# Three of a two-layer decoder kernel's buffers serve as extra slots for the last layer's expert weights, where one did before

## What is computed

```python
def memory_cross_attention(h, mem_n, wq, wkv, wo):
    ...
    s = jnp.einsum('bshd,bmhd->bhsm', q, k).astype(F32) * (X_DH ** -0.5)
    p = jax.nn.softmax(s, axis=-1)
    o = jnp.einsum('bhsm,bmhd->bshd', p, v.astype(F32)).reshape(B, S, D)
    return o.astype(h.dtype) @ wo

def hierarchical_moe(h, w_rg, w_re, w_gate, w_up, w_down):
    ...
    hg = jnp.einsum('nd,edf->nef', t, w_gate)
    hu = jnp.einsum('nd,edf->nef', t, w_up)
    act = (jax.nn.silu(hg.astype(F32)) * hu.astype(F32) * gates[..., None]).astype(t.dtype)
    y = jnp.einsum('nef,efd->nd', act, w_down)
```

## Time and profile before

| | us |
|---|---|
| median of 3 runs | 1109.47 |
| lowest and highest | 1107.93, 1112.87 |
| profiled execution, device time | 1111.42 |
| profiled execution, its span | 1109.5 |
| PE, DVE and ACT busy in the span | 1029.5, 397.4, 136.9 |

### The profile page before, as it was taken

The page is one execution under the profiler, slowest core; times in us unless marked ns, Lnnn a source line. Parts: engine busy times, 40 slices in busy tenths (PEclk is TensorE's granted clock), DMA queues, the critical chain, the costliest instruction groups (busy, mean ns, idle before and its releaser), DMA issues.

```text
span 1109.5 us, 10478 instructions
## 1 busy us (share of the span) xinstructions
PE 1029.5 (93%) x4366; PEld 559.1 (50%) x4366; DVE 397.4 (36%) x722; ACT 136.9 (12%) x303; POOL 58.0 (5%) x105
## 2 busy tenths in 40 slices
PE   6999999999978999999997999999996899988995
PEld 5666556577564443333333855566853433333332
DVE  5203455413133223333243324562124333333332
ACT  4010002302010001100111000041111000100001
POOL 3001111000010000000000101100000100000000
PEclk9999999999998999999998999999999899999998
DMA  8954423252156999999899344226403699999993
GB/s 344 429 223 152 152 84 147 76 195 109 34 215 228 380 429 426 411 428 410 366 425 427 131 152 152 76 79 227 151 2 152 246 431 426 426 426 429 426 426 133
DMA packets 25239, 293.54 MB, mean 265 GB/s; under 512 B 3296, under 2 KB 3552, under 8 KB 8544
## 3 DMA queue, kind: packets, MB, share of 16 engines
q1 hardware_dynamic: 19392, 266.40, 59.0%
q10 hardware_dynamic: 4640, 22.19, 5.2%
q0 software_dynamic: 1152, 4.19, 1.0%
HBM read 283.33 MB, written 9.44 MB: 264 GB/s over the span
## 4 chain that ended last, share of the span: by engine, by line
PE 81%; DMA 11%; DVE 4%; issue 2%; ACT 1%; DVEq 0%; POOL 0%; SPq 0%; ACTq 0%
PE bank L806 14%; PE bank L477 12%; PE bank L830 10%; PE bank L625 10%; PE bank L485 9%; DMA ring<-in_w_experts 8%; PE bank L496 5%; PE bank L498 5%; PE bank L836 4%; PE bank L554 3%; DMA late<-in_w_experts 2%; PE bank L467 2%; PE bank L677 1%; PE bank L690 1%; PE bank L706 1%
## 5 line engine op out<-in xcount | busy, mean ns | idle before, releaser
L806 PE MATMUL bank<-ring,hT 128*64 128x512 f32 x944 | 224.3, 594 | 11.7 <-DMA ring<-in_w_experts 9.8
L806 PEld LDWEIGHTS bank<-ring,hT 128*64 128x64 f32 x944 | 73.8, 137 | 144.1 <-issue 143.0
L477 PE MATMUL bank<-ring,hT 128*128 128x512 f32 x320 | 140.3, 592 | 0.0
L830 PE MATMUL bank<-ring,work 128*64 128x512 f32 x480 | 113.4, 595 | 6.5 <-ACT work L1039 3.2
L625 PE MATMUL bank<-ring,hT 128*128 128x512 f32 x256 | 112.1, 594 | 0.0
L485 PE MATMUL bank<-hT,ring 128*128 128x256 f32 x448 | 99.8, 385 | 2.1 <-DVE hT L1281 2.1
L477 PEld LDWEIGHTS bank<-ring,hT 128*128 128x128 f32 x320 | 59.6, 190 | 68.0 <-issue 67.9
L485 PEld LDWEIGHTS bank<-hT,ring 128*128 128x128 f32 x448 | 86.4, 194 | 14.7 <-DVE hT L1281 2.7
L1562 DVE TENSOR_TENSOR x<-bank,x 128x512 f32<-128x512 f32 x64 | 44.3, 692 | 137.3 <-PE bank L836 137.3
L625 PEld LDWEIGHTS bank<-ring,hT 128*128 128x128 f32 x256 | 48.0, 190 | 57.7 <-issue 56.8
L830 PEld LDWEIGHTS bank<-ring,work 128*64 128x64 f32 x480 | 36.4, 137 | 68.3 <-issue 58.4
(11 more groups left out here) (235 smaller groups left out, 977.9 us busy)
## 6 DMA issues: line engine op xcount, KB each, us to landing
ring<-in_w_experts SPq DMA_DIRECT2D x89, 2048.0 KB, 15.7
ring<-in_w_mix SPq DMA_DIRECT2D x30, 2048.0 KB, 9.2
late<-in_w_experts SPq DMA_DIRECT2D x7, 2048.0 KB, 20.8
late<-in_w_mix ACTq DMA_DIRECT2D x4, 2048.0 KB, 12.5
rot<-by_slot ACTq DMA_DIRECT2D x14, 512.0 KB, 10.5
by_slot<-late ACTq DMA_DIRECT2D x1, 4096.0 KB, 50.3
work<-in_mem SPq DMA_DIRECT2D x2, 512.0 KB, 4.4
x<-in_x SPq DMA_DIRECT2D x1, 1024.0 KB, 13.4
```

The lines of the kernel that those rows point to most:

```text
L477: last = nc.tensor.matmul(b[:, :], lhs[:, c, m * P:(m + 1) * P], w[:, c, :], start=(c == 0), stop=(c == C - 1))
L806: last = nc.tensor.matmul(banks[2 + g][b2 * CAP:(b2 + 1) * CAP, :], rowsT[p % 2][:, c, b2 * CAP:(b2 + 1) * CAP], w, start=(c == 0), stop=( ...
L830: last = nc.tensor.matmul(banks[5 + n][b2 * CAP:(b2 + 1) * CAP, :], ractT[:, c, b2 * CAP:(b2 + 1) * CAP], w, start=(c == 0), stop=(c == 3))
```

## The change

The diff makes `KT` and `memT` one buffer, `keys`, of exactly one slot's size, and lets the last layer's expert units use it as slot `KEYS`, and `work` as slot `WORK`. There are nine slots for these 48 units instead of seven: of each nine units the first goes to `late`, the sixth to `keys`, the seventh to `work`, the others round the ring. The first load into `keys` waits for the job `sx11`, the first into `work` for `pt11`. As `work` is no longer free in the last layer's experts, their temporaries lie in `Vx` there (and one of the dense branch in `rot`). In the first layer all stays where it was. The lines that do the same for the dense branch are left out.

```diff
@@ -35,7 +35,8 @@
 
 
 SLOTS = 6
-LATE = SLOTS
+LATE, KEYS, WORK = SLOTS, SLOTS + 1, SLOTS + 2
+LAST_SLOTS = {0: LATE, 5: KEYS, 6: WORK}
 UNITS = ["k0", "k1", "v0", "v1", "hf", "hq", "hi", "aq", "ak", "hg", "av", "o0", "o1", "q0", "q1", "p0", "p1"]
 KV_UNITS = 4
 PAIRS = N_EXPERTS // 2
@@ -109,11 +110,13 @@
 def unit_places():
 
 
+
     order = []
     for layer in range(DEPTH):
         order += [(layer, name, None) for name in UNITS[KV_UNITS if layer else 0:]]
-        n = SLOTS + (layer == DEPTH - 1)
-        order += [(layer, (j // 6, j % 6), LATE if n > SLOTS and j % n == 0 else None) for j in range(6 * PAIRS)]
+        more = LAST_SLOTS if layer == DEPTH - 1 else {}
+        n = SLOTS + len(more)
+        order += [(layer, (j // 6, j % 6), more.get(j % n)) for j in range(6 * PAIRS)]
     places, at, tenants = {}, 0, {}
     for layer, key, slot in order:
         if slot is None:
@@ -177,7 +180,8 @@
         x = sb("x", [P, M, D])
         xs = sb("xs", [P, M, D])
         hT = sb("hT", [P, C, T])
-        memT = sb("memT", [P, C, T])
+        keys = sb("keys", [P, 2, C, T])
+        memT, KT = keys[:, 0, :, :], keys[:, 1, :, :]
         late = sb("late", [P, 4 * M * W])
         hi = late[:, 0:M * W].rearrange("p (m n) -> p m n", m=M)
         gg = late[:, M * W:2 * M * W].rearrange("p (m n) -> p m n", m=M)
@@ -189,7 +193,6 @@
         S01 = PT[:, 2, 0:HG_HEADS, :]
         PT0 = PT[:, 0:2, :, :].rearrange("p a (h m) t -> p (a h) m t", m=M)
         PT1 = PT[:, 2, :, :]
-        KT = sb("KT", [P, 8, T])
         Vx = sb("Vx", [P, M, D])
         lev = sb("lev", [P, 8, P])
         bias0 = sb("bias0", [P, P])
@@ -236,7 +239,7 @@
         banks = [ctx.enter_context(nc.psum_tensor(f"bank{i}", [P, W], F32)) for i in range(8)]
 
 
-        loaded = [sem(f"loaded{s}") for s in range(SLOTS + 1)]
+        loaded = [sem(f"loaded{s}") for s in range(SLOTS + len(LAST_SLOTS))]
         kv_loaded, kv_done, kv_emptied = sem("kv_loaded"), sem("kv_done"), sem("kv_emptied")
         router_loaded = sem("router_loaded")
         late_reset = sem("late_reset")
@@ -318,7 +321,9 @@
             eng.wait_ge(empt[who], L * EMPTIED[who] + NTH[name])
 
         def slot_view(slot):
-            return ring[:, slot, :] if slot < SLOTS else late[:, 0:C * W]
+            if slot < SLOTS:
+                return ring[:, slot, :]
+            return {LATE: late[:, :], KEYS: keys[:, :, :, :].rearrange("p a c t -> p (a c t)"), WORK: E}[slot]
 
         def unit(name, L=0):
             return slot_view(PLACES[L, name][0]).rearrange("p (c n) -> p c n", c=C)
@@ -341,9 +346,12 @@
             tots.append(TOT[:, :, off:off + (T >> j)])
             off += T >> j
 
-        actb = work[:, 0, :].rearrange("p (m n) -> p m n", m=M)
-        actT = work[:, 1, 0:W].rearrange("p (c t) -> p c t", c=4)
-        gexp = work[:, 2, :].rearrange("p (m n) -> p m n", m=M)
+        def last(L):
+            return L == DEPTH - 1
+
+        actb_of = [(Vx[:, 0, :] if last(L) else work[:, 0, :]).rearrange("p (m n) -> p m n", m=M) for L in range(DEPTH)]
+        gexp_of = [(Vx[:, 1, :] if last(L) else work[:, 2, :]).rearrange("p (m n) -> p m n", m=M) for L in range(DEPTH)]
+        actT_of = [(rot[:, 0:W] if last(L) else work[:, 1, 0:W]).rearrange("p (c t) -> p c t", c=4) for L in range(DEPTH)]
         HALF_PI = float(np.pi / 2)
 
         logits = wsm[:, 0:40].rearrange("p (m n) -> p m n", m=M)
@@ -371,7 +379,9 @@
         by_slot = nc.dram_tensor("by_slot", (N_EXPERTS * CAP, D), F32, kind="Internal").ap()
         rowsT = [hT[:, :, 0:P], hT[:, :, P:T]]
         rows = [rot[:, 0:D], rot[:, D:2 * D]]
-        ract, ractT, rexp = work[:, 0, 0:W], work[:, 1, 0:W].rearrange("p (c t) -> p c t", c=4), work[:, 2, 0:W]
+        ract_of = [Vx[:, 0, 0:W] if last(L) else work[:, 0, 0:W] for L in range(DEPTH)]
+        rexp_of = [Vx[:, 1, 0:W] if last(L) else work[:, 2, 0:W] for L in range(DEPTH)]
+        ractT_of = [(Vx[:, 0, W:D] if last(L) else work[:, 1, 0:W]).rearrange("p (c t) -> p c t", c=4) for L in range(DEPTH)]
         yrows = PT[:, 2, :, :].rearrange("p h t -> p (h t)")
         hot = PT[:, 0, 0:2, :]
         gated = PT[:, 0, 2:4, :]
@@ -414,8 +424,8 @@
 
                 slot, _, had = PLACES[L, key]
                 if had is None:
-                    if slot == LATE:
-                        wait_job(sp, L, "ap1")
+                    if slot >= SLOTS:
+                        wait_job(sp, L, {LATE: "ap1", KEYS: "sx11", WORK: "pt11"}[slot])
                     return
                 l, old = had
                 if isinstance(old, tuple):
@@ -816,7 +826,7 @@
                         rows_transposes(p + 1, 0)
                     pe.wait_ge(r_act[L], p + 1)
                     for k in range(4):
-                        last = nc.tensor.transpose(banks[4][:, k * P:(k + 1) * P], ract[:, k * P:(k + 1) * P], ident[:, :])
+                        last = nc.tensor.transpose(banks[4][:, k * P:(k + 1) * P], ract_of[L][:, k * P:(k + 1) * P], ident[:, :])
                     routed_job(last)
                     if p + 1 < PAIRS:
                         rows_transposes(p + 1, 1)
@@ -827,7 +837,7 @@
                         for c in range(4):
                             for b2 in range(2):
                                 w = expert_unit(p, 4 + b2)[:, c * D + n * W:c * D + (n + 1) * W]
-                                last = nc.tensor.matmul(banks[5 + n][b2 * CAP:(b2 + 1) * CAP, :], ractT[:, c, b2 * CAP:(b2 + 1) * CAP],
+                                last = nc.tensor.matmul(banks[5 + n][b2 * CAP:(b2 + 1) * CAP, :], ractT_of[L][:, c, b2 * CAP:(b2 + 1) * CAP],
                                                         w, start=(c == 0), stop=(c == 3))
                         routed_job(last)
                     for n in range(2):
...
@@ -1032,11 +1042,11 @@
 
                 def routed(p):
                     act.wait_ge(r_jobs[L], ROUTED[p, "gate"])
-                    nc.scalar.activation(rexp, banks[2][:, :], ACT.Exp, scale=-1.0).then_inc(r_gexp[L], 1)
+                    nc.scalar.activation(rexp_of[L], banks[2][:, :], ACT.Exp, scale=-1.0).then_inc(r_gexp[L], 1)
                     act.wait_ge(r_jobs[L], ROUTED[p, "weights"])
                     nc.scalar.activation(gatedT, banks[7][:, 0:M * P].rearrange("p (m t) -> p m t", m=M), ACT.Copy).then_inc(r_evac[L], 1)
                     act.wait_ge(r_jobs[L], ROUTED[p, "act"])
-                    nc.scalar.activation(ractT, banks[4][:, :].rearrange("p (c t) -> p c t", c=4), ACT.Copy).then_inc(r_evac[L], 1)
+                    nc.scalar.activation(ractT_of[L], banks[4][:, :].rearrange("p (c t) -> p c t", c=4), ACT.Copy).then_inc(r_evac[L], 1)
                     if p + 3 < PAIRS:
                         act.wait_ge(r_jobs[L], ROUTED[p, "rows1"])
                         load_rows(p + 3)
...
@@ -1546,11 +1556,11 @@
 
                     taken(r_jobs[L], ROUTED[p, "gate"])
                     dve.wait_ge(r_gexp[L], p + 1)
-                    inner.link(V.tensor_scalar(rexp, rexp, 1.0, None, ALU.add))
-                    inner.link(V.reciprocal(rexp, rexp))
-                    inner.link(V.tensor_tensor(rexp, banks[2][:, :], rexp, ALU.mult))
+                    inner.link(V.tensor_scalar(rexp_of[L], rexp_of[L], 1.0, None, ALU.add))
+                    inner.link(V.reciprocal(rexp_of[L], rexp_of[L]))
+                    inner.link(V.tensor_tensor(rexp_of[L], banks[2][:, :], rexp_of[L], ALU.mult))
                     taken(r_jobs[L], ROUTED[p, "up"])
-                    V.tensor_tensor(ract, banks[3][:, :], rexp, ALU.mult).then_inc(r_act[L], 1)
+                    V.tensor_tensor(ract_of[L], banks[3][:, :], rexp_of[L], ALU.mult).then_inc(r_act[L], 1)
                     if p + 1 < PAIRS:
                         for c2 in range(2):
                             rows_transposed(p + 1, c2, ROUTED[p, f"rows{c2}"])
...
```

More of the change, by code:

```diff
@@ L859, in dense @@
                             for k in range(4):
-                                last = nc.tensor.transpose(banks[4][:, k * P:(k + 1) * P], actb[:, m, k * P:(k + 1) * P], ident[:, :])
+                                last = nc.tensor.transpose(banks[4][:, k * P:(k + 1) * P], actb_of[L][:, m, k * P:(k + 1) * P], ident[:, :])
                             last.then_inc(d_jobs[L], 1)
@@ L868, in dense @@
                                 for c in range(4):
-                                    last = nc.tensor.matmul(banks[5 + n][:, :], actT[:, c, :], w[:, c, n * W:(n + 1) * W],
+                                    last = nc.tensor.matmul(banks[5 + n][:, :], actT_of[L][:, c, :], w[:, c, n * W:(n + 1) * W],
                                                             start=(c == 0), stop=(c == 3))
@@ L1054, in dense @@
                             act.wait_ge(d_act[L], n4 + 2 * b2)
-                            nc.scalar.activation(gexp[:, m, :], banks[m][:, :], ACT.Exp, scale=-1.0).then_inc(d_gexp[L], 1)
```

(7 more changed lines are left out.)

## The result

| | before | changed |
|---|---|---|
| first measurement, median of 4 runs, us | 1110.65 (1107.93 to 1112.87) | 1100.89 (1099.52 to 1101.56) |
| ratio of the changed kernel to the one before | | 0.9909, 95% interval 0.9887 to 0.9931 |
| second measurement, median of 11 and of 6 runs, us | 1111.15 | 1102.24 (1099.26 to 1105.85) |
| its ratio | | 0.9922, interval 0.9898 to 0.9946 |
| profiled execution, device time and span, us | 1111.42, 1109.5 | 1101.56, 1099.7 |

The changed kernel is faster by 0.9%, some 9.8 us in the first measurement and 8.9 in the second. The forecast was 9.8 us and 1099.7 us.

The account below looks back on a forecast made before the run. The prediction took the last layer's full stream of expert loads, ending with unit 47, as the bound. Parts 1, 2 and 5 gave 0, the stream -9.78: 1109.47 - 9.8 = 1099.7 us, range 1095 to 1104.7.

Parts of the forecast that it names:

- What bounds the kernel: Last layer's experts: the landing of unit 47, at 1088.51 us in a gapless stream of 4.89 us a unit, sets the end.
- Part 1 and 2: Idle stretch before the experts: units 5 and 6 load early into `keys` (805.64 us) and `work` (812.4 us), cost 0.
- Part 3: Stream after 877.32 us: 39 units to draw instead of 41, so unit 47 lands at 1078.73 us, -9.78 us.
- Part 4: Last pairs: PE is ready for down at 1078.1 us, DMA still ends last by 0.6; some 5 us of waits stay.
- rival A: Experts: PE becomes the bound in all pairs, no DMA wait left, -14.1 us, 1095.4 us; chance 0.05.
- Part 5: Experts' temporaries in `Vx` and the merged buffer: only addresses differ, cost 0.
- The median: Whole run: 1109.47 us, the median before, less 9.8 gives 1099.7 us.
- B: Rival, expert stream: a slot filled late or a gap leaves one unit's gain, -4.9 us, 1104.6 us; chance 0.05.
- C: Rival, end of the chain: early loads happen but something else holds the last down products, 1109.5 us; chance 0.07.
- D: Rival: loads outside the ring are slow, 1140.7 us, chance 0.03; elsewhere D means first gate products to last down products' start.

Follow-up runs that it names:

- work alone: Changed kernel without the slot `keys`: eight slots, unit 5 going to `work`; ratio 0.9967 to the kernel before.
- keys alone: Changed kernel without the slot `work`: eight slots, unit 5 going to `keys`; ratio 0.9963 to the kernel before.
- the held one: Changed kernel with the first load into `work` also waiting for the first pair's gate products, six units loaded ahead; ratio 1.0050 to the kernel before.

## Why the prediction was right

**What bounds the kernel** was right. The landing of the last unit ended the chain before and after.

**Part 1 and 2, the slots.** Each took a unit's 4.9 us off D, alone and together, and both new loads lie in the stretch that was idle. What they need from that stretch is only that it comes before the first gate job: with the first load into `work` held back past it, the gain turned into a loss.

**Part 3, the stream.** Unit 47 was to land 1078.73 - 870.14 = 208.6 us after the first gate products. In the changed kernel it did so at 1044.94 + 31.83 - 868.23 = 208.5.

**Part 4, what is late next.** Waits of about 5 us were to stay, and 5.0 stayed; pair 6's up products were to begin 1039.6 - 870.14 = 169.5 us after the first gate products and did so at 1037.78 - 868.23 = 169.6. The wait before the last down products was put at 0.6 us and was 1.1. The bound by PE was put at 14.1 us below the kernel before (rival A) and was measured at 14.45. So what these two slots leave is 4.6 us, whichever way it is sought: finer waits were tried and brought 2.9 of them, a third slot was not tried.

**Part 5, the temporaries** at 0: measured 1.0002, and 0.16 us in D.

**The median** was forecast at 1099.7 and measured at 1100.89. The 1.2 us between them come from the starting point: the forecast took off from a median of 1109.47, and with one run more the kernel before had 1110.65. That the difference of the medians, 9.76 us, is so near to the 9.8 forecast is in part luck, as the second measurement gave 8.91. In the profiled executions two things that no step of the sum holds happened to cancel: the first gate products began 1.9 us sooner than in the earlier trace rows, and the last down products took 1.7 us longer. By the part of the run that the change touches, the gain is 9.84 us to the last down products and 8.15 or 9.65 us (first and second profile) to the last sums.

**The rivals.** A did not happen; PE waits for loads in pairs 6 and 7 still. B fell with the two kernels of one slot each, and C with the changed kernel's own profile, where the last down products began 9.84 us sooner after the first gate products. D (slow buffers) fell with the kernels of one slot, and with the rows of 423 GB/s over a stream of which eight units went to `keys` and `work`. (B's 1104.7 as the end of the range is 1104.6 by its own sum, 1109.47 - 4.89; nothing hangs on it.)

The prediction set the measured rate against the 358 GB/s that the Trainium skill gives for a core ("DMA: Bandwidth & Descriptors", section Specifications), and called the two at odds. They are not. The Trainium skill, "HBM Reference", section Specifications (TRN2), calls the 358 GB/s the share of each core when both cores on a memory stack are streaming, and puts a core alone at about 425 GB/s. One core ran here, and the trace agrees with that second figure: 423 GB/s over 173 us.

## What to carry to other kernels

When a stretch is bound by a full stream of loads, its end moves by what is loaded before it, so look for buffers that are dead by then and for an idle stretch ahead in which to fill them; depth that can't be filled in time is worth nothing. Price it as units x time per unit, and check at once how far the compute engine is behind the stream, as that is where the gain stops (here 14.4 us, of which two slots took 9.8). When only a few waits for whole loads are left at the end, load just those in halves: a unit in halves cost the stream up to 0.1 us here, which the last pair alone pays back. In all pairs halves did not pay, in part because their order held back a load that had a free slot: whenever the order of a queue is changed, look again for what now stands behind a wait.

## What the runs showed of the hardware

**TensorE's clock can fall in the middle of a pair that waits for loads.** The last down products of the changed kernel took 8.79 us in its first profile; the windows around that place:

```profile
1070.00:1077.00 7.00, 5.34 (x28) 2.13 (x26) 1.20 (x2) 0.98 (x2) 0.00 (x0) 1.00 0.72 304
1077.00:1081.00 4.00, 4.00 (x12) 1.46 (x14) 0.00 (x0) 0.00 (x0) 0.00 (x0) 0.57 0.00 0
1081.00:1086.00 5.00, 5.00 (x23) 1.85 (x20) 0.00 (x0) 0.88 (x2) 0.00 (x0) 1.00 0.00 0
```

The granted clock is 0.57 over the 4 us after the last wait, so mostly at the lower of the two levels (1.2 of 2.4 GHz), and full on both sides. PE had waited 1.8 us before the last up products and 1.1 us before the down products. The same dip came in the kernel with units 1 and 2 in the new slots (8.78 us), and at earlier pairs in the kernel with the temporaries only (8.80 us at 986.88), in keys alone and in the held one; there the time was taken up again by the wait for the next load. It did not come in the kernel before, in work alone, in the second profile of the changed kernel, in any with halves, or in the one whose pairs wait for no load. So it came only in executions with such waits, but not in each of them (the one execution without them is little to go by), and one in the last pair costs 1.7 us. What decides it stays open.

**The scatter of whole runs comes from before the change's place.** Over the 13 profiled executions the first gate products of the last layer began between 866.48 and 872.63 us, though nothing that is computed before them differs; the kernel before ran between 1105.72 and 1115.14 us. What comes after E is all but fixed: device time less that start and less E is 11.9 to 12.4 us in all 13. What makes the start vary stays open. D repeats far better: 208.67, 208.85 and 208.94 us in three executions of the same nine filled slots.

**SP's issuing slowed when many loads were outstanding on its queue.** In the last layer's experts of the changed kernel most loads of 2 MB took 0.33 to 0.53 us to issue, and one 0.82, with some six ahead of them (31.83 us to land, at 4.89 each). With 1 MB loads behind one another in the last two pairs, the issue itself took 2.1 us:

```profile
1018.28 2.79 SPq L479 DMA_DIRECT2D keys<-in_w_experts  x1
1021.12 2.14 SPq L479 DMA_DIRECT2D ring<-in_w_experts  x1
```

In the kernel with halves in all pairs eight issues in a row, from 1029.61 to 1049.51 us, took 2.49 us each on average (one of them 6.30), and the stream needs 2.4 to 2.5 us for 1 MB. So there the queue took in a new load about as one went out. It did little harm here: from 1030 to 1079 us of the kernel with halves in two pairs the DMA share was 0.99, at 411 GB/s.
